# Index queries by columns for the later rows, key and head weights on their own, row squares from the input's columns

## The chip, the cores and the metric

The kernel runs on 1 core of one Trainium2 chip. The metric is the device time of one execution in microseconds (us), median of the runs. TensorE's matmuls are PE in the profile, its weight loads PEld; VectorE is DVE, ScalarE is ACT, GpSimd is POOL, SyncE is SP.

## What is computed

One decoder layer on 256 rows of width 2048, all in float32. What matters here:

```python
h = rms_norm(x, norm_gain)                 # 256 x 2048
proj = h @ w_in                            # split into qa ka va ga | qi ki wi | qb kb vb gb | ma mb
qi = apply_rope(qi.reshape(S, 16, 64)); ki = apply_rope(ki)      # index queries, one shared key
score = sum over heads of relu(qi_h . ki) * wi_h                 # 256 x 256, causal
_, sel = top_k(score, 64)                  # topk = SEQ // 4: each row attends to 64 keys of branch A
```

qi has 1024 columns of w_in, ki 64 and the head weights wi 16. A row with at most 64 keys before it (rows 0 to 63) selects all of them, whatever its scores. Branch A attends to the selected keys, branch B to all; both are gated, projected, merged and projected again.

## The kernel before

**Products.** w_in is read in units: two tiles of 128 rows of w_in (k) by up to 512 columns. Eight units (CK) make a chunk over all 2048 rows. Each operand is split into `hi`, rounded to the type in which TensorE takes a matmul of 4-byte data in one pass, and `lo`, what is left. A unit is three products (hi x hi, lo x hi, hi x lo) for 2 k tiles and 2 blocks of rows: 12 matmuls. h stands transposed (`hT_hi`, `hT_lo`) and is the stationary operand; the weights stream by as the moving one, so a chunk comes out with rows on partitions. Products for which this isn't done (the early rows' scores, the values of branch A) are plain float32.

**Order.** SP loads unit u into slot u % 4 of `raw` (a ring of four), ACT makes `hi` (`make_hi`), DVE `lo` (`make_lo`), TensorE multiplies. ACT makes unit u's `hi` only when unit u-4 is multiplied (`unit_done`), so all engines step with TensorE. The loops `for c ... for i in range(CK)` on each engine write out by hand which other work stands ahead of which unit; `make_hi_ahead(c, i)` and `make_lo_ahead(c, i)` make the unit four further on.

**The index part.** Chunks 0, 1 and 2 are 384, 384 and 336 columns wide (`IDX_W`): queries in six, and in the last four heads, the key and the head weights beside them (`KIWI` = 80 columns). Chunks 0 and 1 are interleaved at first (`FIRST_UNITS`), with the products in an order that lets them start early (`early_unit`), since x lands meanwhile. ACT takes each chunk out of PSUM to `stage`, DVE ropes it (`index_rope`), TensorE transposes it (`transpose_roped`, blocks of 128), ACT and DVE take out `qk_hi` and `qi_lo`. `index_scores` uses them much later, in chunks 12 and 14. Chunks 3 to 10 are qa, ka, qb, kb (`C_QK` = 3), each normed per head and roped (`norm_rope`) while the next is multiplied; then values, gates, merge gates, attention beside them, and the output projections.

**Row norms.** x comes transposed (`x_columns`), and is multiplied by the gain before the product; the factor 1/rms of each row (`rstd`) is applied when chunks are taken out. For it x is loaded once more by rows (`x_own`, 2 MB), and ACT squares and sums it, 2048 columns at a time.

Of the kernel before, what the change touches and what calls it, by code (L numbers as in the profile page):

```python
# [11 lines left out]
P = 128  # L31
D = 2048
# [17 lines left out]
X_OWN_AFTER = ((1, 3), (1, 5), (1, 7), (2, 1))  # L50
# [4 lines left out]
IDX_W = (384, 384, 256 + KIWI)  # L55
IDX_BLOCKS = tuple(w // P for w in IDX_W)
# [13 lines left out]
C_QK, C_V, C_G, C_M = 3, 11, 15, 19  # L70
C_O = 27
# [21 lines left out]
FIRST_UNITS = ((0, 0), (1, 0), (0, 1), (1, 1)) + tuple((c, i) for c in range(2) for i in range(2, CK))  # L93
FIRST_END = CK + 2
assert IDX_W[0] == IDX_W[1]


def chunk_end(c):
    return FIRST_END if isinstance(c, int) and c == 0 else c * CK + CK


def chunk_width(c):
    return IDX_W[c] if c < C_QK else CW

# [24 lines left out]
def chunk_bank(c):  # L129

    return 2 * ((c + 1) % 2)


def build_layer(nc, x, x_columns, positions, w_in, a_q_gain, a_k_gain, b_q_gain, b_k_gain,
# [4 lines left out]
    with ExitStack() as ctx:  # L139
# [29 lines left out]
        x_own = sb("x_own", [P, RT, D], at=qk_at + 4 * 24 * S)  # L169
# [17 lines left out]


# [6 lines left out]
        def of_four(n, part, home):  # L195
            maps = home[:, :, :].rearrange("p r (j s) -> p j r s", s=CW)
            first = {0: 0, 1: 0, 2: 4, 3: 4}[(n - C_QK) // 2] + 2 * ((n - C_QK) % 2)
            return maps[:, first:first + 2, :, part]

        def of_blocks(n, cols, home):  # L200
            at = (n - C_QK) * 4 + QA
            return home[:, at:at + 4, cols].rearrange("p (a b) s -> p a b s", b=2)
# [72 lines left out]
        tab_ci = g[:, 1, 0:128].rearrange("p (r d) -> p r d", r=RT)  # L275
        tab_si = g[:, 1, 128:256].rearrange("p (r d) -> p r d", r=RT)
# [10 lines left out]
        x_own_landed = [sem(f"x_own_landed_{r}") for r in range(RT)]  # L287
# [18 lines left out]
        index_tables_ready, tables_ready = sem("index_tables_ready"), sem("tables_ready")  # L306
        lam_sums, lam_exps = sem("lam_sums"), sem("lam_exps")
        x_squares, rstd_ready = sem("x_squares"), sem("rstd_ready")

# [22 lines left out]
        def _(sp):  # L332
# [4 lines left out]
            def load_x_own(part):  # L337
                r, at = part // 2, slice((part % 2) * (D // 2), (part % 2 + 1) * (D // 2))
                sp.dma_start(x_own[:, r, at], x_rows[:, r, at]).then_inc(x_own_landed[r], 16)

            def load_first(u, j):
                c, i = FIRST_UNITS[u]
                col = COL["qi"] + c * IDX_W[0]
                sp.dma_start(raw[:, u, j, 0:IDX_W[0]],
                             w_in[0][(2 * i + j) * P:(2 * i + j + 1) * P, col:col + IDX_W[0]]
                             ).then_inc((raw_first[u], raw_landed[u])[j], 16)

            def load(slot, u, weights, k0, col, width=CW):
# [3 lines left out]
                src = weights[0][k0 * P:(k0 + 2) * P, bass.ds(col, width)].rearrange("(k p) n -> p k n", p=P)  # L352
                sp.dma_start(raw[:, slot, :, 0:width], src).then_inc(raw_landed[slot], 16)

            def load_chunk(c, col, width=CW):
                for i in range(CK):
                    load(i % RING, c * CK + i, w_in, 2 * i, col, width)


# [3 lines left out]
            for u in range(1, EARLY):  # L363
                if u > 1:
                    load_x(u)
                load_first(u, 0)
                load_first(u, 1)
            for u in range(EARLY, 2 * CK):
# [3 lines left out]
                load(u % RING, u, w_in, 2 * i, COL["qi"] + c * IDX_W[0], IDX_W[0])  # L372
# [5 lines left out]
            rows = [(gains[:, j], row) for j, row in enumerate((a_q_gain, a_k_gain, b_q_gain, b_k_gain))]  # L378
            rows += [(lams[:, j], row) for j, row in enumerate((lambda_q1, lambda_k1, lambda_q2, lambda_k2))]
            rows += [(sub_gain[:, :], b_subln_gain)]  # L380
            for c, col in ((2, COL["qi"] + IDX_W[0] + IDX_W[1]),):
                for i in range(CK):
                    load(i % RING, c * CK + i, w_in, 2 * i, col, IDX_W[c])
                    if (c, i) in X_OWN_AFTER:
                        load_x_own(X_OWN_AFTER.index((c, i)))
                    for to, row in rows[i:i + 1] if c == 2 and i < CK - 1 else rows[i:] if c == 2 else ():
                        sp.dma_start(to, row[0].partition_broadcast(P)).then_inc(consts_landed, 16)
            with sp.Fori(0, 2) as branch:
                with sp.Fori(0, 4) as n:
                    load_chunk(C_QK + branch * 4 + n, branch * COL["qb"] + n * CW)  # L390
# [34 lines left out]
        def _(pool):  # L425
            nc.gpsimd.memset(ident[:, :], 0.0).then_inc(pool_wrote, 1)
            nc.gpsimd.memset(bias_b[:, :], 0.0).then_inc(pool_wrote, 1)
            nc.gpsimd.memset(half[:, :], -0.5).then_inc(pool_wrote, 1)
            pool.wait_ge(pool_wrote, 3)
# [57 lines left out]
            rows = [[t[:, r * 64:(r + 1) * 64] for t in (cos_t, nsin_t, sin_t)] for r in range(RT)]  # L487
            for r, (c_r, *s_r) in enumerate(rows):
                for b in range(2):
                    half_b = slice(b * 32, b * 32 + 32)  # L490
                    nc.gpsimd.tensor_copy(tab_ci[:, r, half_b], c_r[:, 0:64:2]).then_inc(index_tables_ready, 1)
                    nc.gpsimd.tensor_copy(tab_si[:, r, half_b], s_r[b][:, 0:64:2]).then_inc(index_tables_ready, 1)
# [22 lines left out]
        def _(pe):  # L515
            mm = nc.tensor.matmul

            def unit(u, slot, k0, s_hi, s_lo, bank, first, last, width=CW):

                w_hi, w_lo = (t[:, slot, :, 0:width] for t in (hi, lo))  # L520
                pe.wait_ge(lo_ready, u + 1)
                order = [(j, r) for j in range(2) for r in range(RT)]
                for j, r in order:
                    a_hi = s_hi[:, k0 + j, r * P:(r + 1) * P]
                    a_lo = s_lo[:, k0 + j, r * P:(r + 1) * P]
                    o = ps[:, bank + r, 0:width]
                    mm(o, a_hi, w_hi[:, j], start=first and j == 0, stop=False)  # L527
                    mm(o, a_hi, w_lo[:, j], start=False, stop=False)  # L528
                    ins = mm(o, a_lo, w_hi[:, j], start=False, stop=j == 1 and last)  # L529
                ins.then_inc(unit_done, 1)  # L530

            def early_unit(u):

                c, unit_k = FIRST_UNITS[u]

                def products(stationary, moving, j, first=False, last=False):
                    for r in range(RT):
                        ins = mm(ps[:, chunk_bank(c) + r, 0:IDX_W[0]], stationary[:, 2 * unit_k + j, r * P:(r + 1) * P],  # L538
                                 moving[:, u % RING, j, 0:IDX_W[0]], start=first, stop=last)
                    return ins  # L540

                for j in range(2):
                    pe.wait_ge(hi_first if j == 0 and u < EARLY else hi_ready, u + 1)
                    pe.wait_ge(x_hi_first if j == 0 and u == 0 else split_hi, unit_k + 1)
                    products(hT_hi, hi, j, first=unit_k == 0 and j == 0)
                    pe.wait_ge(x_lo_first if j == 0 and u == 0 else split_lo, unit_k + 1)
                    products(hT_lo, hi, j)
                for j in range(2):
                    pe.wait_ge(lo_first if j == 0 and u == 0 else lo_ready, u + 1)
                    ins = products(hT_hi, lo, j, last=unit_k == CK - 1 and j == 1)  # L550
                ins.then_inc(unit_done, 1)

            def w_in_unit(c, i, bank, width=CW):

                if not isinstance(c, int) or c >= 2:
                    if i == 0:
                        pe.wait_ge(chunk_out, c - 1)
# [855 lines left out]
```

## Time and profile before

| | |
|---|---|
| median of 3 runs | 798.16 us (797.63 to 798.37) |
| span of the profiled execution, first to last instruction | 796.4 us |
| PE, PEld busy | 792.7 us, 667.3 us |
| DVE, ACT, POOL busy | 481.5, 418.4, 46.8 us |
| read from HBM | 150.25 MB, 191 GB/s over the span |

The profile was taken from one execution; what lies outside its span is the difference to a run's time. A matmul's printed duration has its whole pipeline in it, so several overlap: what one costs in a stream is the distance from its start to the next one's. TensorE's granted clock is 1.00 (2.4 GHz) over the kernel.

### The profile page before, as it was taken

Reading aid. Unit: us, or ns where it says so; the run is one execution under the profiler, and the core shown is the slowest. Engines: PE = TensorE matmul, PEld = TensorE weight load, DVE = VectorE, ACT = ScalarE, POOL = GpSimd, SP = SyncE. Lnnn points to the kernel's source line nnn. Section 1 sums busy time; section 2 is a strip of 40 time slices with the busy share of each in tenths; the row PEclk is TensorE's granted clock in tenths of the full one; section 3 lists DMA queues with packets and bytes.
Section 4 is the critical chain, followed back from the end, with each engine's and each line's share of the span. In section 5 each row is a group of like instructions: output and inputs, shape, how many; then the busy total and the mean of one; then the engine's idle time right before and its main releaser. Section 6 shows DMA issues by size and latency. Waiting matters only on the chain.

```text
span 796.4 us, 10773 instructions
## 1 busy us (share of the span) xinstructions
PE 792.7 (100%) x3810; PEld 667.3 (84%) x3810; DVE 481.5 (60%) x663; ACT 418.4 (53%) x670; POOL 46.8 (6%) x70
## 2 busy tenths in 40 slices
PE   9999999999999999999999999999999999999998
PEld 9998888888888888888888888888888888888887
DVE  7677766666677554668656455555455566665453
ACT  7574556665555454556465554555575444443431
POOL 4341000000000000000000000000000000000000
PEclk9999999999999999999999999999999999999999
DMA  9986665666666565666655665655665855555563
GB/s 316 313 264 198 186 187 168 183 199 180 199 187 187 171 194 162 196 189 193 177 154 173 166 176 161 185 160 172 173 185 182 293 195 184 185 194 189 187 194 122
DMA packets 81082, 152.92 MB, mean 192 GB/s; under 512 B 5136, under 2 KB 12944, under 8 KB 80784
## 3 DMA queue, kind: packets, MB, share of 16 engines
q1 hardware_dynamic: 80752, 152.06, 62.8%
q8 instruction: 25, 0.41, 0.2%
q10 hardware_dynamic: 288, 0.30, 0.1%
q14 instruction: 17, 0.14, 0.0%
HBM read 150.25 MB, written 2.10 MB: 191 GB/s over the span
## 4 chain that ended last, share of the span: by engine, by line
PE 97%; ACT 1%; DMA 1%; SPq 0%; issue 0%; DVE 0%; ACTq 0%
PE ps L527 30%; PE ps L529 30%; PE ps L528 29%; PE ps L538 2%; PE ps L569 1%; PE ps L580 1%; DMA raw<-in_w_in 1%; PE ps L638 0%; PE ps L749 0%; PE ps L748 0%; PE ps L747 0%; PE ps L646 0%; ACT L938 0%; ACT L832 0%; ACT g L832 0%; PE ps L626 0%
## 5 line engine op out<-in xcount | busy, mean ns | idle before, releaser
L1068 DVE TENSOR_TENSOR lo<-raw,hi 128x1024 fp32r<-128x1024 f32 (+2 forms) x279 | 335.2, 1204 | 290.2 <-ACT hi L819 288.4
L819 ACT ACTIVATE hi<-raw 128x1024 fp32r<-128x1024 f32 (+2 forms) x277 | 287.1, 1040 | 337.4 <-PE ps L529 323.8
L527 PE MATMUL ps<-hi,hT_hi 128*128 128x512 f32 (+2 forms) x936 | 364.3, 389 | 0.0
L529 PE MATMUL ps<-hi,hT_lo 128*128 128x512 f32 (+2 forms) x936 | 361.1, 386 | 0.0
L528 PE MATMUL ps<-lo,hT_hi 128*128 128x512 f32 (+2 forms) x936 | 360.8, 385 | 0.0
L529 PEld LDWEIGHTS ps<-hi,hT_lo 128*128 128x128 f32 x936 | 175.7, 188 | 35.1
L528 PEld LDWEIGHTS ps<-lo,hT_hi 128*128 128x128 f32 x936 | 175.8, 188 | 32.9
L527 PEld LDWEIGHTS ps<-hi,hT_hi 128*128 128x128 f32 x936 | 175.7, 188 | 33.0
L527 PE MATMUL ps<-hi,ogT_hi 128*128 128x512 f32 x128 | 50.1, 391 | 0.0
L529 PE MATMUL ps<-hi,ogT_lo 128*128 128x512 f32 x128 | 49.8, 389 | 0.0
L528 PE MATMUL ps<-lo,ogT_hi 128*128 128x512 f32 x128 | 49.8, 389 | 0.0
L453 POOL TENSOR_SCALAR small<-small 128x8 f32<-128x8 f32 (+1 forms) x13 | 2.8, 212 | 504.2 <-ACT stage L999 318.4
L529 PEld LDWEIGHTS ps<-hi,ogT_lo 128*128 128x128 f32 x128 | 24.0, 188 | 5.0
L528 PEld LDWEIGHTS ps<-lo,ogT_hi 128*128 128x128 f32 x128 | 24.0, 188 | 4.9
L527 PEld LDWEIGHTS ps<-hi,ogT_hi 128*128 128x128 f32 x128 | 24.0, 188 | 4.9
L938 ACT ACTIVATE roped<-stage,small 128x128 f32<-128x128 f32 (+1 forms) x32 | 14.3, 446 | 13.0 <-DVE small L1206 13.0
L856 ACT ACTIVATE swapped<-stage 128x128 f32<-128x128 f32 x64 | 18.9, 297 | 0.3
L455 POOL TENSOR_TENSOR small<-small,half 128x8 f32<-128x8 f32 (+1 forms) x13 | 16.6, 1281 | 1.1
L1088 DVE TENSOR_TENSOR swapped<-stage,g 128x256 f32<-128x256 f32 (+2 forms) x44 | 16.2, 409 | 0.0
L1084 DVE TENSOR_TENSOR roped<-stage,g 128x512 f32<-128x512 f32 (+2 forms) x22 | 14.5, 660 | 0.0
L1092 DVE TENSOR_TENSOR roped<-roped,swapped 128x1024 f32<-128x1024 f32 (+2 forms) x11 | 12.3, 1121 | 0.0
L856 ACT ACTIVATION_READ_ACCUMULATOR swapped<-stage 128x1 f32 x64 | 12.0, 188 | 0.0
(167 smaller groups left out, 484.5 us busy)
## 6 DMA issues: line engine op xcount, KB each, us to landing
raw<-in_w_in SPq DMA_DIRECT2D x192, 512.0 KB, 3.8
raw<-in_w_out SPq DMA_DIRECT2D x32, 512.0 KB, 4.3
raw<-in_w_o_a SPq DMA_DIRECT2D x16, 512.0 KB, 3.7
raw<-in_w_o_b SPq DMA_DIRECT2D x16, 512.0 KB, 3.6
raw<-in_w_in SPq DMA_DIRECT2D x13, 384.0 KB, 5.3
raw<-in_w_in SPq DMA_DIRECT2D x8, 336.0 KB, 5.3
x_own<-in_x SPq DMA_DIRECT2D x4, 512.0 KB, 6.4
g<-in_x SPq DMA_DIRECT2D x1, 2048.0 KB, 10.3
```

The lines of the kernel that those rows point to most:

```text
L455: return tt(out, mean, half[:, 0:width], ALU.pow)
L527: mm(o, a_hi, w_hi[:, j], start=first and j == 0, stop=False)
L528: mm(o, a_hi, w_lo[:, j], start=False, stop=False)
L529: ins = mm(o, a_lo, w_hi[:, j], start=False, stop=j == 1 and last)
L538: ins = mm(ps[:, chunk_bank(c) + r, 0:IDX_W[0]], stationary[:, 2 * unit_k + j, r * P:(r + 1) * P], moving[:, u % RING, j, 0:IDX_W[0]], sta ...
L819: activation(hi[:, slot, :, 0:width], raw[:, slot, :, 0:width], ACT.Copy).then_inc(hi_ready, 1)
L856: ins = activation(swapped[:, r, at], stage[:, r, at], ACT.Square, accum_out=ss_h[:, j:j + 1])
L938: ins = activation(probs[buf][:, at], masked[buf][:, at], ACT.Exp, scale=SCALE, bias=neg_max[:, j:j + 1], accum_out=sum_p[:, j:j + 1])
L1068: tt(lo[:, slot, :, 0:width], raw[:, slot, :, 0:width], hi[:, slot, :, 0:width].bitcast(F32), ALU.subtract).then_inc(lo_ready, 1)
L1084: mark(tt(cos_out[:, r], src[:, r], c_tab, ALU.mult))
L1088: mark(tt(sin_out[:, r, :, half_b], src[:, r, :, other], s_tab, ALU.mult))
L1092: tt(roped[:, :, 0:cols], roped[:, :, 0:cols], swapped[:, :, 0:cols], ALU.add).then_inc(rope_done, 1)
```

## The change

- The queries are computed transposed, and for rows 64 to 255 alone (`Q_FIRST` = 64, `Q_LATE` = 192): 128 columns of w_in are the stationary operand and 192 columns of hT stream by. Two halves of 512 columns, `query_unit`, 24 matmuls a unit. ACT copies them out with halves of heads swapped (`swap_queries`), DVE ropes them in place (`query_rope`) with tables that TensorE has transposed (`transpose_tables`). No transposes of queries. Their first 64 rows are zeros, and `bias_a` is cleared for those rows ahead of the selection's use. 1/rms isn't applied to the queries, as before.
- qa's first chunk is moved to the front and interleaved with the first half of the queries; `C_QK` is now 2.
- The key and head weights (80 columns) are loaded once (`kw`), split, and multiplied in `key_products`, two k tiles ahead of each unit of chunk 3.
- The row squares come from x_columns: ACT squares eight pieces of 512, POOL adds them up (`sq`), TensorE sums over partitions (`sum_squares`). `x_own` is gone.

```diff
-IDX_W = (384, 384, 256 + KIWI)
-IDX_BLOCKS = tuple(w // P for w in IDX_W)
+Q_FIRST = TOPK
+Q_LATE = S - Q_FIRST
+QI_BLOCKS = IDX_HEADS * IDX_DIM // P // 2
...
-C_QK, C_V, C_G, C_M = 3, 11, 15, 19
-C_O = 27
+C_QK, C_V, C_G, C_M = 2, 10, 14, 18
+C_O = 26
...
-FIRST_UNITS = ((0, 0), (1, 0), (0, 1), (1, 1)) + tuple((c, i) for c in range(2) for i in range(2, CK))
-FIRST_END = CK + 2
+FIRST_UNITS = tuple((c, i) for i in range(CK) for c in range(2))
+FIRST_END = 2 * CK
+QI_BANKS = (2, 4)
...
@@ SP @@
-                if (c, i) in X_OWN_AFTER:
-                    load_x_own(X_OWN_AFTER.index((c, i)))
...
+                if i == 2:
+                    src = w_in[0][:, COL["kiwi"]:COL["kiwi"] + KIWI].rearrange("(k p) n -> p k n", p=P)
+                    sp.dma_start(kw[:, :, :], src).then_inc(kw_landed, 16)
...
@@ POOL @@
+            nc.gpsimd.memset(qkT[:, QI:QI + 2 * QI_BLOCKS, 0:Q_FIRST], 0.0).then_inc(qi_cleared, 1)
...
+            for t in range(1, CK):
+                pool.wait_ge(x_squared, t + 1)
+                mark(tt(sq[:, 0, :], sq[:, 0, :], sq[:, t, :], ALU.add))
+                settle()
+            tt(sq[:, 0, 0:S], sq[:, 0, 0:S], sq[:, 0, S:2 * S], ALU.add).then_inc(x_summed, 1)
...
@@ TensorE @@
+            def query_unit(u, i, eight):
...
+                def products(weights, moving, first=False, last=False):
+                    for j in range(2):
+                        for b in range(QI_BLOCKS):
+                            o = ps[:, QI_BANKS[eight] + b // 2, b % 2 * Q_LATE:(b % 2 + 1) * Q_LATE]
+                            ins = mm(o, weights[:, u % RING, j, b * P:(b + 1) * P], moving[:, 2 * i + j, Q_FIRST:S],
+                                     start=first and j == 0 and b % 2 == 0, stop=last and j == 1, skip_group_check=True)
+                    return ins
...
+                products(hi, hT_hi, first=i == 0)
+                products(hi, hT_lo)
+                pe.wait_ge(lo_ready, u + 1)
+                products(lo, hT_hi, last=i == CK - 1).then_inc(unit_done, 1)
+
+            def key_products(i):
+
+                if i == 0:
+                    pe.wait_ge(kw_lo_ready, 1)
+                    pe.wait_ge(tabT_ready, 1)
+                for k in (2 * i, 2 * i + 1):
+                    for r in range(RT):
+                        a_hi, a_lo = (t[:, k, r * P:(r + 1) * P] for t in (hT_hi, hT_lo))
+                        o = ps[:, S0, r * P:r * P + KIWI]
+                        mm(o, a_hi, kw_hi[:, k, :], start=k == 0 and r == 0, stop=False, skip_group_check=True)
+                        mm(o, a_hi, kw_lo[:, k, :], start=False, stop=False, skip_group_check=True)
+                        ins = mm(o, a_lo, kw_hi[:, k, :], start=False, stop=k == KT - 1, skip_group_check=True)
...
+            def transpose_tables():
...
+                pe.wait_ge(index_tables_ready, 3 * RT)
...
+            def sum_squares():
...
+                pe.wait_ge(x_summed, 1)
+                pe.wait_ge(tabT_ready, 1)
+                for r in range(RT):
+                    ins = mm(ps[:, S0 + 1, 2 * r:2 * r + 2], sq[:, 0, r * P:(r + 1) * P], ones, start=True, stop=True)
...
             for u, (c, i) in enumerate(FIRST_UNITS):
...
+                if u == 11:
+                    transpose_tables()
+                if c == 0:
+                    early_unit(u, i)
                 else:
+                    query_unit(u, i, 0)
+            for i in range(CK):
+                if i == 2:
+                    sum_squares()
+                query_unit(2 * CK + i, i, 1)
+            for c in range(C_QK + 1, C_QK + 4):
                 for i in range(CK):
+                    if i == 6:
+                        transpose_roped(c - 1 - C_QK)
+                    if c == C_QK + 1:
+                        key_products(i)
+                    if (c, i) == (C_QK + 3, 2):
+                        transpose_index_key()
+                    w_in_unit(c, i, chunk_bank(c))
...
@@ ScalarE @@
+                if c == 1:
+                    square_x(i)
+                if u == 11:
                     act.wait_ge(reduced, 1)
                     activation(sin_t, ang, ACT.Sin).then_inc(sin_ready, 1)
...
+                    if c in (C_QK, C_QK + 1) and i < 4:
+                        swap_queries(c - C_QK, i)
+                    if c in (C_QK, C_QK + 1) and i == 6:
+                        queries_hi(c - C_QK)
+                    if (c, i) == (C_QK, 6):
+                        act.wait_ge(kw_landed, 16)
+                        activation(kw_hi[:, :, :], kw[:, :, :], ACT.Copy).then_inc(kw_hi_ready, 1)
...
@@ VectorE @@
+                    if c in (C_QK, C_QK + 1) and 4 <= i <= 5:
+                        for step in ((0, 1), (2,))[i - 4]:
+                            query_rope(c - C_QK, step)
+                    if c in (C_QK, C_QK + 1) and i == 7:
+                        query_rope(c - C_QK, 3)
+                    if (c, i) == (C_QK, 7):
+                        dve.wait_ge(kw_hi_ready, 1)
+                        tt(kw_lo[:, :, :], kw[:, :, :], kw_hi[:, :, :].bitcast(F32), ALU.subtract).then_inc(kw_lo_ready, 1)
...
+                        mark(nc.vector.memset(bias_a[0:Q_FIRST, 0:P], 0.0))
```

`query_rope` has four steps: two products from PSUM with the cosines and one of `qi_swap` with the sines (the third signals `qi_read`), the sum (256 elements into `qkT`, 512 in `qi_rope`), and later the low part (512). `swap_queries` copies one quarter of the partitions, 768 elements.

## Rows read from the trace of the kernel before

**Rows 1.** Page of the profile, busy time and the chain that ended last.

```profile
PE 792.7 (100%) x3810; PEld 667.3 (84%) x3810; DVE 481.5 (60%) x663; ACT 418.4 (53%) x670; POOL 46.8 (6%) x70
...
PE 97%; ACT 1%; DMA 1%; SPq 0%; issue 0%; DVE 0%; ACTq 0%
```

**Rows 2.** Index part: PE, PEld, DVE, ACT, POOL busy, granted clock, DMA share, GB/s.

```profile
4.68:54.53 49.85, 49.77 (x302) 49.29 (x301) 38.34 (x59) 36.78 (x59) 18.48 (x29) 1.00 0.96 310
```

**Rows 3.** Groups by shape, TensorE, 4.6 to 54.6 us: the index products.

```profile
L538 PE MATMUL ps<-hi,hT_hi 128*128 128x384 f32 x40 | 10.6, 345 | 0.1
L527 PE MATMUL ps<-hi,hT_hi 128*128 128x336 f32 x32 | 10.2, 320 | 0.0
...
L527 PE MATMUL ps<-hi,hT_hi 128*128 128x384 f32 x24 | 8.0, 334 | 0.0
```

**Rows 4.** Timeline of TensorE: start us, us, line, shape; five stretches.

```profile
33.01 0.33 PE L527 MATMUL ps<-hi,hT_hi 128*128 128x384 f32 x1
...
38.55 0.34 PE L529 MATMUL ps<-hi,hT_lo 128*128 128x384 f32 x1
...
52.69 0.32 PE L527 MATMUL ps<-hi,hT_hi 128*128 128x336 f32 x1
...
54.38 0.32 PE L529 MATMUL ps<-hi,hT_lo 128*128 128x336 f32 x1
...
72.12 0.39 PE L527 MATMUL ps<-hi,hT_hi 128*128 128x512 f32 x1
...
83.92 0.39 PE L528 MATMUL ps<-lo,hT_hi 128*128 128x512 f32 x1
...
487.37 0.28 PE L665 MATMUL ps<-qk_hi,swapped_r 128*128 128x256 f32 x1
...
488.32 0.28 PE L667 MATMUL ps<-qk_hi,pT_lo 128*128 128x256 f32 x1
...
405.75 0.38 PE L653 MATMUL ps<-v,swapped 128*128 128x128 f32 x2
405.97 0.39 PE L654 MATMUL ps<-v,swapped 128*128 128x128 f32 x2
```

**Rows 5.** Timeline of TensorE's weight loads after short work, two places.

```profile
93.82 0.19 PEld L527 LDWEIGHTS ps<-hi,hT_hi 128*128 128x128 f32 x1
93.92 0.19 PEld L528 LDWEIGHTS ps<-lo,hT_hi 128*128 128x128 f32 x1
...
262.33 0.19 PEld L527 LDWEIGHTS ps<-hi,hT_hi 128*128 128x128 f32 x1
262.44 0.19 PEld L528 LDWEIGHTS ps<-lo,hT_hi 128*128 128x128 f32 x1
```

**Rows 6.** Timeline of TensorE: six index transposes and the matmul behind them.

```profile
38.73 0.63 PE L569 MATMUL ps<-ident_r,roped_r 128*128 128x128 f32 x6
39.20 0.39 PE L527 MATMUL ps<-hi,hT_hi 128*128 128x336 f32 x1
```

**Rows 7.** Groups by shape, ACT and DVE, 4.6 to 60 us.

```profile
L819 ACT ACTIVATE hi<-raw 128x1024 fp32r<-128x1024 f32 x5 | 5.3, 1058 | 1.8 <-PE ps L529 1.3 <-DMA raw<-in_w_in 0.5
...
L1068 DVE TENSOR_TENSOR lo<-raw,hi 128x1024 fp32r<-128x1024 f32 x5 | 6.7, 1340 | 3.6 <-ACT hi L819 3.6
...
L1092 DVE TENSOR_TENSOR roped<-roped,swapped 128x768 f32<-128x768 f32 x2 | 1.9, 948 | 0.0
L1137 DVE TENSOR_TENSOR g_r<-ps,qk_hi 128x384 fp32r<-128x384 f32 x2 | 1.1, 549 | 0.0
```

**Rows 8.** Timeline of ACT in the chunk from 77 us: a split that waits.

```profile
85.31 1.06 ACT L819 ACTIVATE hi<-raw 128x1024 fp32r<-128x1024 f32 x1 [1.56 <-PE ps L529]
```

**Rows 9.** Timeline of POOL: two table products of one size.

```profile
50.91 1.74 POOL L500 TENSOR_TENSOR g<-v 128x256 f32<-128x256 f32 x1
...
57.67 0.74 POOL L500 TENSOR_TENSOR g<-v 128x256 f32<-128x256 f32 x1
```

**Rows 10.** Timeline of TensorE: its first product of weights.

```profile
4.68 0.80 PE L538 MATMUL ps<-hi,hT_hi 128*128 128x384 f32 x2
```

More of the change, by code:

```diff
@@ L371, in _ @@
                     load_x(i + 1)
[L372 removed]
+                load(u % RING, u, w_in, 2 * i, COL[("qa", "qi")[c]])
                 if u == EARLY + 1:
                     sp.dma_start(pos_i[:, :], positions).then_inc(phases_landed, 16)
[L375 to L390 removed]
+                if u >= 2 * CK - 4:
+                    load_row(u - (2 * CK - 4))
+            for i in range(CK):
+                load(i % RING, 2 * CK + i, w_in, 2 * i, COL["qi"] + CW)
+                if i < 5:
+                    load_row(4 + i)
+                if i == 2:
+                    src = w_in[0][:, COL["kiwi"]:COL["kiwi"] + KIWI].rearrange("(k p) n -> p k n", p=P)
+                    sp.dma_start(kw[:, :, :], src).then_inc(kw_landed, 16)
+            with sp.Fori(1, 4) as n:
+                load_chunk(C_QK + n, n * CW)
+            with sp.Fori(0, 4) as n:
+                load_chunk(C_QK + 4 + n, n * CW + COL["qb"])
             for c, name in ((C_V, "va"), (C_V + 2, "vb"), (C_G, "ga"), (C_G + 2, "gb")):
@@ L516, in _, with unit @@
             mm = nc.tensor.matmul
-            def unit(u, slot, k0, s_hi, s_lo, bank, first, last, width=CW):
-                w_hi, w_lo = (t[:, slot, :, 0:width] for t in (hi, lo))
+            def unit(u, slot, k0, s_hi, s_lo, bank, first, last):
                 pe.wait_ge(lo_ready, u + 1)
@@ L549, in early_unit @@
                     pe.wait_ge(lo_first if j == 0 and u == 0 else lo_ready, u + 1)
-                    ins = products(hT_hi, lo, j, last=unit_k == CK - 1 and j == 1)
+                    ins = products(hT_hi, lo, j, last=i == CK - 1 and j == 1)
                 ins.then_inc(unit_done, 1)
[L553 to L557, printed above, removed]
-                    unit(c * CK + i, i % RING, 2 * i, hT_hi, hT_lo, bank, i == 0, i == CK - 1, width)
@@ L562, in transpose_roped, with w_in_unit @@
+            def w_in_unit(c, i, bank):
+                if i == 0:
+                    if isinstance(c, int) and c == C_QK + 1:
+                        pe.wait_ge(qi_read, 1)
+                    else:
+                        pe.wait_ge(chunk_out, taken_out(c - 2))
+                unit(c * CK + i, i % RING, 2 * i, hT_hi, hT_lo, bank, i == 0, i == CK - 1)
+            def transpose_roped(n):
                 pe.wait_ge(rope_done, n + 1)
-                if not isinstance(n, int) or n > 0:
+                if isinstance(n, int) and n == 0:
+                    pe.wait_ge(qi_read, 2)
+                else:
@@ new lines, in queries_hi, with key_out @@
+            def queries_hi(eight):
+                act.wait_ge(qi_roped, eight + 1)
+                first = QI + eight * QI_BLOCKS
+                activation(qk_hi[:, first:first + QI_BLOCKS, P:S], qi_rope[:, :, P - Q_FIRST:Q_LATE],
+                           ACT.Copy).then_inc(qi_hi_ready, 1)
+            def key_out():
+                act.wait_ge(kw_done, 1)
+                act.wait_ge(rstd_ready, 1)
+                for r in range(RT):
+                    ins = activation(kst[:, r, :], ps[:, S0, r * P:r * P + KIWI], ACT.Copy, scale=rstd[:, r:r + 1])
+                ins.then_inc(kst_out, 1)
```

446 lines of the change are left out of this document (238 added, 208 removed).

## The prediction

> **What bounds the kernel now.** I read the page first. TensorE is busy 100% of the span and 97% of the chain that ended last is its matmuls [rows 1]; VectorE at 60% and ScalarE at 53% are covers. So whatever adds or takes TensorE time moves the end one for one, and every other engine counts only if it makes TensorE wait. Then I asked for the stretch of the index projection, from the first product of weights to the first 512-wide chunk: 49.85 us, no idle TensorE to speak of, granted clock 1.00, DMA at 96% of its engines but still ahead [rows 2]. The reader is to see that the stretch is a plain sum of matmuls: three products of 40 + 24 matmuls of 384 columns, three of 32 of 336 columns [rows 3], so 192 and 96.
>
> The duration printed for a matmul (0.33 to 0.39) contains its pipeline; what counts is the distance from start to start. 32 distances at 384 columns take 5.54 us, 0.173 each; 11 at 336 take 1.69, 0.154; 52 at 512 take 11.80, 0.227; 8 at 256 take 0.95, 0.119 [rows 4]. That is 0.42 ns a column and 12 ns for each matmul (0.227 - 0.173 over 128 columns, and the rest). 192 x 0.173 + 96 x 0.154 = 33.2 + 14.8 = 48.0 us. That is what is replaced.
>
> The price of a narrow matmul is not in that line, for each one also loads its own 128x128 weights, and at 256 columns and more this is hidden. Where a load finds the spare place free, two follow one another by 0.10 and by 0.11 us [rows 5] (93.82 to 93.92, behind short transposes; 262.33 to 262.44, behind the index scores). And the plain f32 products of 128 columns, which show two records and two loads each, take 0.22 us a pair, again 0.11 a load [rows 4]. So below some 230 columns I expect the load to set the pace.
>
> **The change, part by part.**
>
> *Query products.* 2 halves x 8 units x 24 = 384 matmuls of 192 columns. By columns each would be 12 + 192 x 0.42 = 0.093 us; by the load 0.11. The load is the longer, so 384 x 0.11 = 42.2 us.
>
> *Key and head weights on their own.* 16 row tiles x 2 x 3 = 96 matmuls of 80 columns, which until now rode along in the 336-wide ones for 80 x 0.42 = 34 ns each, 3.2 us in all. Alone, each costs a load: 96 x 0.11 = 10.6 us. Together 52.8 against 48.0: **+4.8 us**. This is the heart of it: a quarter of the columns goes (106,000 to 81,400), but the number of matmuls goes from 288 to 480. Bounds of the price: 0.105 from the shorter distance between loads, 0.12 if the 12 ns of every matmul come on top of the load (which is the 256-wide row): 480 x 0.105 = 50.4 (+2.4), 480 x 0.12 = 57.6 (+9.6). I take 0.11, since the plain f32 pairs show it in a stream.
>
> The two distances of rows 5 agree with the Trainium skill, "TensorE: Matmul & The Clock Gate", section "LDWEIGHTS (loading the stationary operand)", which gives columns over 1.2 GHz, 107 ns for 128; by it 480 x 0.107 = 51.4 us would be the two parts, +3.4.
>
> *Transposes.* Six take 0.47 us until the next matmul starts (38.73 to 39.20) [rows 6], 0.078 each. 18 (16 of queries, 2 of keys) become 6 (4 of tables, 2 of keys): **-0.9**.
>
> *Row squares.* Two plain f32 products of 2 columns, four loads: **+0.4**. The two ScalarE squares of 2048 columns and x_own's 2 MB go, eight squares of 512 come. DMA and ScalarE there don't bound [rows 1, 2]: nothing. Its cover gone would show as ScalarE splitting late; rings of four units (10 us) stand between.
>
> *qa's first chunk* only moves to the front; its 96 matmuls stay 512 wide: nothing. At the start the first transfers are a third larger (512 for 384 columns) and TensorE begins at 4.68 us when they are there [rows 10]: I estimate **+0.3**, 0 to 1.
>
> *A new wait.* key_products(0) stands in TensorE's order at the head of chunk 3 and waits for kw_lo. Who makes that? Unit n's split on ScalarE (1.06 us for 1024 elements [rows 7]) starts only when unit n-4 is done; the ones of today wait for just that, 1.56 us [rows 8]. In chunk 2, with U24 the end of its last unit: kw_hi (1280 elements, by the 1.06 of 1024 some 1.3 us) stands ahead of the split at i=6, which can start at U23 at the earliest and ends at U23 + 1.1, or 1.4 with queries_hi and kw_hi ahead of it (they start after the split of i=5, U22 + 1.1). VectorE then does that unit's lo (1.2 us by 0.95 for 768, 1.34 beside a busy POOL), the queries' low part (0.7 by 0.55 for 384) and kw_lo (1.4) [rows 7]: U23 + 4.7. A query unit lasts 24 x 0.11 = 2.6 us, so kw_lo is ready at U24 + 2.0, and TensorE stands from U24 on. **+2.0**, from 0 (if VectorE runs ahead) to 3.5. Behind that wait in TensorE's queue is the whole of chunk 3; no one else is hurt, since hi and lo of its units are made meanwhile.
>
> *Other waits.* The first rope of queries has to have read banks 2 and 3 before chunk 3: five units of slack. Transposing qa waits for the second half's rope, but chunk 3 lasts 8 x 1.3 us longer by its key products, more than VectorE's added 2.1 us there (two of 0.55 from PSUM, one of 0.95) [rows 7]. On POOL seven sums of 512 elements precede sum_squares in unit 18, near 53 us. A 256-element product takes 0.74 or 1.74 us, the long ones beside a busy VectorE [rows 9]; so 1.3 to 3 us each. They follow the tables, which follow the sines that ScalarE does after the split of unit 11, so once unit 7 has ended (5 + 4 x (2.7 + 2.6) = 26 us): I estimate 33 us. They end between 43 and 55, and unit 18 starts at 5 + 8 x 5.3 + 2 x 2.6 = 53: mostly in time, and up to 2 us late, for which I leave room in the high bound. The memset of qkT (512 elements) lies in POOL's long wait for positions; the two small VectorE operations by the selection lie ahead of the scores they serve: nothing.
>
> Sum: 4.8 - 0.9 + 0.4 + 0.3 + 2.0 = **+6.6 us**. The profiled execution's span is 796.4, the runs' median 798.16, 1.8 of it outside the span; the forecast is 803.0 for the span, 804.8 for the median. Its own range: +1.9 (price 0.105, no stall, no late start) to +13.6 (0.12, waits of 3.5 in all, start 1): 800 to 812.
>
> **Rivals.**
>
> *Columns decide (ends faster).* If the weight load overlaps wholly with the matmuls before it, several ahead, the pace is 0.093 us at 192 and 0.046 at 80: 35.7 + 4.4 = 40.1 us, -7.9; with the other terms -6.1 us, 792; without the stall 790. It decides once the 480 matmuls cost under 0.096 us on average, where the sum is zero. For it: nothing ever paces TensorE at 256 columns but the columns [rows 4]. Against it: rows 5, where the next load starts only 0.10 to 0.11 after the last although its matmul had begun. By the Trainium skill, "TensorE: Matmul & The Clock Gate", section "Back-to-back issue gap", the distance is N/2.4 + 2.5 ns, 82.5 for 192 and 36 for 80; 31.7 + 3.4 us would be the two parts, and the kernel about 11 us faster. The same section allows more for pairs of load and matmul, and rows 4 already show 119 where it has 109 for 256.
>
> *Narrow rounded products run as plain f32 does.* The narrowest product on split operands in the trace has 256 columns. Plain f32 takes 0.22 for 128 columns [rows 4], four times a column's price. If 192-wide ones fell to that: 384 x 0.33 + 96 x 0.22 = 148 us, +100, 898 us, and no stall for kw. For it only that the trace shows no narrow one; against it that transposes of such operands at 128 columns take 0.078 [rows 6].
>
> *Nothing much.* Price near 0.10 and no stall cancel with the transposes: within 1.6 us of 798.
>
> **Chances.** The load decides 0.72; columns decide 0.12; as plain f32 0.10; cancels 0.06. Under 0.2% (1.6 us) no measurement of this kernel tells from no change. Faster 0.13, same 0.05, slower 0.82. The range takes in the likeliest case and the fast one, 791 to 812, and leaves out the 898.
>
> **What the changed profile would show.** Distance of 0.11 between 192-wide and between 80-wide matmuls alike, with PEld without gaps (right), or 0.093 and 0.046 (columns), or two records each (plain f32). One TensorE gap of some 2 us before the first 80-wide matmul, released by VectorE's kw_lo. sum_squares without a wait for POOL. From chunk 4 on the same distances as now. A different price of a load in a stream, or a drop of the granted clock from 1.00 beside the narrow products, would make the sum wrong.

## The result, and the profile after

The changed kernel takes 811.12 us (median of 4, 810.49 to 811.70), the kernel before 797.97 us in the runs beside it (797.63 to 798.37). The ratio is 1.0166, 95% interval 1.0152 to 1.0180: 13.2 us slower. The forecast was 804.8, slower with 0.82, range 791 to 812. Sign and mechanism came as forecast; the loss is twice the +6.6 us of the sum, at the upper end of the likeliest case's own range (800 to 812). The profiled execution's span is 808.6 us, 12.2 more than before's 796.4; the steps below are counted against that.

The page of the kernel after (busy time, granted clock in 40 slices, chain that ended last by engine), to be held against [rows 1]:

```profile
span 808.6 us, 11086 instructions
PE 801.3 (99%) x3994; PEld 675.1 (83%) x3994; DVE 485.3 (60%) x645; ACT 421.2 (52%) x667; POOL 65.0 (8%) x77
PEclk9998999999999999999999999999999999999999
PE 96%; ACT 2%; DVE 1%; issue 0%; ACTq 0%
```

Two things are new. TensorE's share of the chain is one per cent lower, ScalarE's and VectorE's together two per cent higher: somewhere TensorE waited. And the fourth slice of the granted clock (61 to 81 us) is below full. The waits of the first 110 us name one place (engine and line, what it waited for: us in total, times, longest):

```profile
PE ps L596 <- DVE kw_lo L1305: 3.6, 1, 3.6
```

Two stretches of the kernel after (columns as in [rows 2]):

```profile
4.68:71.50 66.82, 66.82 (x490) 62.20 (x488) 50.20 (x49) 45.30 (x64) 43.49 (x41) 1.00 0.85 268
75.16:81.67 6.51, 6.51 (x22) 5.70 (x23) 1.08 (x1) 2.22 (x16) 1.87 (x2) 0.51 0.48 148
```

Up to 71.5 us, with qa's chunk and all queries in it, TensorE stands nowhere and the granted clock is 1.00. Behind the wait it is 0.51, which is the lower level, 1.2 GHz; from the next slices of the page on it is full again. TensorE's timeline shows the start, the narrow products, the row squares, the wait and what follows it (start us, us, line, shape, and in brackets the idle time before and its releaser):

```profile
4.89 1.22 PE L553 MATMUL ps<-hi,hT_hi 128*128 128x512 f32 x2
...
13.89 1.03 PE L576 MATMUL ps<-hT_hi,hi 128*128 128x192 f32 x8
...
54.88 0.53 PE L617 MATMUL ps<-const-float32-1.0,sq 128*128 128x2 f32 x4
55.27 0.90 PE L576 MATMUL ps<-hT_hi,hi 128*128 128x192 f32 x6
...
60.69 1.05 PE L576 MATMUL ps<-hT_hi,hi 128*128 128x192 f32 x8
61.58 1.05 PE L576 MATMUL ps<-hT_lo,hi 128*128 128x192 f32 x8
...
70.51 1.05 PE L576 MATMUL ps<-hT_hi,lo 128*128 128x192 f32 x8
75.16 0.44 PE L596 MATMUL ps<-kw_hi,hT_hi 128*128 128x80 f32 x1 [3.59 <-DVE kw_lo L1305]
...
77.74 0.77 PE L542 MATMUL ps<-hi,hT_hi 128*128 128x512 f32 x1
...
81.67 0.40 PE L542 MATMUL ps<-hi,hT_hi 128*128 128x512 f32 x1
...
82.61 0.29 PE L596 MATMUL ps<-kw_hi,hT_hi 128*128 128x80 f32 x1
82.72 0.28 PE L597 MATMUL ps<-kw_lo,hT_hi 128*128 128x80 f32 x1
...
83.61 0.47 PE L542 MATMUL ps<-hi,hT_hi 128*128 128x512 f32 x1
83.93 0.39 PE L543 MATMUL ps<-lo,hT_hi 128*128 128x512 f32 x1
```

and, from the kernel before, the first product behind its fourth group of 12:

```profile
13.77 0.51 PE L538 MATMUL ps<-hi,hT_hi 128*128 128x384 f32 x2
```

Read by distances, start to start, as the prediction did:

- Eight query products of 192 columns take 0.89 us (60.69 to 61.58), 0.111 each. 384 of them are 42.7 us. The narrow key products lie 0.11 apart too (82.61 to 82.72), although they have 80 columns. A group of 12 takes 1.25 us (82.36 to 83.61), since the first follows a 512-wide product whose long stay hides part of its load; the 96 are 10.1. The first 512-wide product behind each group then takes 0.32 (83.61 to 83.93) and not 0.23: 0.7 for the eight. Together 53.5 where 48.0 stood: +5.5.
- The row squares take 0.39 us (54.88 to 55.27), with no wait: +0.4. Twelve transposes fewer: -0.9.
- The start: the first product at 4.89, not 4.68 [rows 10]. Up to 13.89, 24 products of 512 columns and 24 of 192 take 9.0 us where their steady distances make 8.13, 0.87 too much. Before, the first 48 products of 384 columns took 9.09 (4.68 to 13.77) where 48 x 0.173 is 8.3, 0.77 too much. Together 0.2 + 0.87 - 0.77 = +0.3.
- The wait: eight products from 70.51 end their turn at 71.4, and the next starts at 75.16. +3.75.
- The granted clock after the wait: 12 key products take 2.58 us (75.16 to 77.74), 0.213 apart instead of 0.112, +1.2. Nine 512-wide ones take 3.93 (77.74 to 81.67) instead of 9 x 0.227 and the 0.09 of the first, 2.13, +1.8. Together +3.0.

5.5 + 0.4 - 0.9 + 0.3 + 3.75 + 3.0 = 12.05 of the 12.2 us. Who was late for the wait is seen on the other engines. VectorE of the kernel after, then ScalarE, then POOL:

```profile
63.18 1.02 DVE L1218 TENSOR_TENSOR qi_rope<-ps,idx_tabT 128x384 f32<-128x384 f32 x2
...
65.29 1.75 DVE L1175 TENSOR_TENSOR lo<-raw,hi 128x1024 fp32r<-128x1024 f32 x1
66.97 0.95 DVE L1228 TENSOR_TENSOR qkT<-qi_rope,qi_swap 128x256 f32<-128x256 f32 x1
67.85 1.22 DVE L1229 TENSOR_TENSOR qi_rope<-qi_rope,qi_swap 128x512 f32<-128x512 f32 x1
...
71.87 1.22 DVE L1175 TENSOR_TENSOR lo<-raw,hi 128x1024 fp32r<-128x1024 f32 x1 [1.12 <-ACT hi L917]
...
73.62 1.48 DVE L1305 TENSOR_TENSOR kw_lo<-kw,kw_hi 128x1280 fp32r<-128x1280 f32 x1
```

```profile
69.10 0.64 ACT L948 ACTIVATE qk_hi<-qi_rope 128x512 fp32r<-128x512 f32 x1 [1.74 <-DVE qi_rope L1229]
69.64 1.26 ACT L1027 ACTIVATE kw_hi<-kw 128x1280 fp32r<-128x1280 f32 x1
```

```profile
35.43 13.07 POOL L506 TENSOR_TENSOR sq<-sq 128x512 f32<-128x512 f32 x7
48.59 1.60 POOL L508 TENSOR_TENSOR sq<-sq 128x256 f32<-128x256 f32 x1
...
61.42 0.73 POOL L516 TENSOR_TENSOR g<-v 128x256 f32<-128x256 f32 x1
```

kw_lo is the last of VectorE's list, as forecast. But ScalarE's `queries_hi` stood 1.74 us for its input `qi_rope`, and `kw_hi` and the split behind it, from 70.80 on, moved with it. `qi_rope` was late because VectorE's operations from 65.29 on ran while POOL made the head's tables (61.42 to 72.2): the low part took 1.75 us instead of the 1.22 it takes at 71.87, the sum of 256 elements 0.95 (the same line took 0.42 for the second half, with POOL idle), the one of 512 took 1.22 (0.69). Each of the three is 0.53 longer, 1.6 us in all. With the one at 64.23, which took 1.14 instead of the 0.96 of its twin at 98.16, that is 1.8 us, all of ScalarE's wait of 1.74.

### The profile page after: what moved, and what is told of

The parts are those of the page before. It is cut to its first block, busy times and chain, and to the rows that moved or that the text cites. A ratio compares the mean times of both kernels' runs of the same rounds, so it can differ in the third digit from the quotient of the medians.

```text
span 808.6 us, 11086 instructions
## 1 busy us (share of the span) xinstructions
PE 801.3 (99%) x3994; PEld 675.1 (83%) x3994; DVE 485.3 (60%) x645; ACT 421.2 (52%) x667; POOL 65.0 (8%) x77
## 4 chain that ended last, share of the span: by engine, by line
PE 96%; ACT 2%; DVE 1%; issue 0%; ACTq 0%
PE ps L542 27%; PE ps L544 27%; PE ps L543 27%; PE ps L576 4%; PE ps L553 3%; PE ps L643 1%; PE ps L660 1%; PE ps L666 1%; ACT hi L917 1%; PE ps L597 0%; PE ps L598 0%; PE ps L596 0%; PE ps L733 0%; PE ps L843 0%; PE ps L842 0%
## 5 line engine op out<-in xcount | busy, mean ns | idle before, releaser
L1175 DVE TENSOR_TENSOR lo<-raw,hi 128x1024 fp32r<-128x1024 f32 x271 | 336.5, 1245 | 295.9 <-ACT hi L917 294.3
L917 ACT ACTIVATE hi<-raw 128x1024 fp32r<-128x1024 f32 x269 | 283.5, 1058 | 345.4 <-PE ps L544 326.4
L542 PE MATMUL ps<-hi,hT_hi 128*128 128x512 f32 x848 | 334.8, 395 | 0.0
L544 PE MATMUL ps<-hi,hT_lo 128*128 128x512 f32 x848 | 331.1, 390 | 0.0
L543 PE MATMUL ps<-lo,hT_hi 128*128 128x512 f32 x848 | 331.1, 390 | 0.0
L544 PEld LDWEIGHTS ps<-hi,hT_lo 128*128 128x128 f32 x848 | 159.6, 188 | 34.1
L576 PE MATMUL ps<-hT_hi,lo 128*128 128x192 f32 x128 | 16.9, 274 | 0.0
L576 PE MATMUL ps<-hT_lo,hi 128*128 128x192 f32 x128 | 16.9, 274 | 0.0
L576 PE MATMUL ps<-hT_hi,hi 128*128 128x192 f32 x128 | 16.8, 274 | 0.0
L576 PEld LDWEIGHTS ps<-hT_hi,hi 128*128 128x128 f32 x128 | 16.1, 191 | 0.5
```

The source lines that it names most:

```text
L542: mm(o, a_hi, hi[:, slot, j, :], start=first and j == 0, stop=False)
L543: mm(o, a_hi, lo[:, slot, j, :], start=False, stop=False)
L544: ins = mm(o, a_lo, hi[:, slot, j, :], start=False, stop=j == 1 and last)
L576: ins = mm(o, weights[:, u % RING, j, b * P:(b + 1) * P], moving[:, 2 * i + j, Q_FIRST:S], start=first and j == 0 and b % 2 == 0, stop=las ...
L917: activation(hi[:, slot, :, :], raw[:, slot, :, :], ACT.Copy).then_inc(hi_ready, 1)
L1175: tt(lo[:, slot, :, :], raw[:, slot, :, :], hi[:, slot, :, :].bitcast(F32), ALU.subtract).then_inc(lo_ready, 1)
```

## The experiments

**Undo the lateness of kw alone.** ScalarE's split moves four units ahead, and VectorE's with it:

```diff
@@ ScalarE @@
-                    if (c, i) == (C_QK, 6):
+                    if (c, i) == (C_QK, 2):
                         act.wait_ge(kw_landed, 16)
@@ VectorE @@
-                    if (c, i) == (C_QK, 7):
+                    if (c, i) == (C_QK, 3):
                         dve.wait_ge(kw_hi_ready, 1)
```

> The split of the key and head weights is made four and five units earlier (their transfer had landed near 48 us). Theory: the wait of 3.6 us goes, and with it the half clock that followed it (about 3.0 us), so 6.6 us less than the changed kernel, near 804.5, ratio to the kernel before 1.008. Rival 1: the half clock comes from the narrow products and not from the wait: it stays, 3.6 us less, 807.5. Rival 2: another late step of VectorE takes the wait's place: less than 3 us gained, with a TensorE gap of over 1 us elsewhere.

Measured: 803.56 us (803.45 to 803.97), ratio to before 1.0068 (1.0051 to 1.0085), 7.6 us under the kernel after; span 802.0. TensorE's timeline at the same place:

```profile
70.50 1.05 PE L576 MATMUL ps<-hT_hi,lo 128*128 128x192 f32 x8
71.40 0.22 PE L596 MATMUL ps<-kw_hi,hT_hi 128*128 128x80 f32 x1
71.45 0.28 PE L597 MATMUL ps<-kw_lo,hT_hi 128*128 128x80 f32 x1
```

The first key product starts at 71.40 instead of 75.16, the next ones follow 0.11 apart at full clock, and no wait of TensorE is left. The spans differ by 6.6, the two terms above make 6.75. (The medians differ by 7.6, because the changed kernel's profiled execution was its shortest run.) So one late input of 1280 elements cost more than half of the whole loss. What is left, +5.6 of span, is the products, the start, the squares and the transposes: 5.5 + 0.3 + 0.4 - 0.9 = 5.3.

**Idle time, or narrow products, as the cause of the lower clock.** The wait stays, and TensorE multiplies zeros into an unused part of a bank meanwhile:

```diff
                 if i == 0:
+                    for _ in range(16):
+                        mm(ps[:, S0 + 1, P:2 * P], zeros, zeros, start=True, stop=True)
                     pe.wait_ge(kw_lo_ready, 1)
```

> The wait stays, but 16 products of zeros (3.5 us) stand in it. Theory: the idle time is what lowered the clock, so it stays at 1.00 after it: 3.0 us less than the changed kernel, near 808. Rival: the narrow products lower it, so nothing changes (811).

Measured: 807.57 us (807.50 to 807.81), ratio 1.0119 (1.0102 to 1.0136); span 805.6. Its timeline, and below it the stretch around it:

```profile
71.15 3.76 PE L591 MATMUL ps<-const-float32-0.0 128*128 128x128 f32 x32
74.90 0.30 PE L598 MATMUL ps<-kw_hi,hT_hi 128*128 128x80 f32 x1
75.03 0.28 PE L599 MATMUL ps<-kw_lo,hT_hi 128*128 128x80 f32 x1
```

```profile
71.00:90.00 19.00, 19.00 (x126) 17.09 (x126) 11.87 (x15) 11.64 (x27) 2.79 (x4) 1.00 0.48 140
```

The same narrow products stand here, no earlier than VectorE allows, but the clock stays at 1.00, and the span is 3.0 under that of the kernel after. The first 12 key products and nine 512-wide ones behind them take 3.51 us instead of 6.51. So it was the idle TensorE and not the narrowness of what follows that brought the lower level, and its price is 3.0 us, beside the wait's own 3.6 (805.6 against 802.0 for the first experiment).

**Load or columns as the pace.** Two widths beside the kernel's 192. In one, all but the first query product of each block have 128 columns; in the other all have 256:

```diff
@@ 128 columns @@
+                            width = Q_LATE if first else P
+                            o = ps[:, QI_BANKS[eight] + b // 2, (b % 2 + 1) * Q_LATE - width:(b % 2 + 1) * Q_LATE]
+                            ins = mm(o, weights[:, u % RING, j, b * P:(b + 1) * P], moving[:, 2 * i + j, S - width:S],
@@ 256 columns @@
+                            o = ps[:, QI_BANKS[eight] + b // 2, b % 2 * S:(b % 2 + 1) * S]
+                            ins = mm(o, weights[:, u % RING, j, b * P:(b + 1) * P], moving[:, 2 * i + j, 0:S],
```

> The query products take 128 columns in place of 192 (all but the first product of each block; the queries of 64 rows are left incomplete). Theory, the weight load sets the pace: distances stay at 0.111 us, total within 0.5 us of the changed kernel. Rival, columns set it: 368 x 64 x 0.42 ns = 9.9 us less.

> The query products take all 256 columns (what is read of them afterwards is at the wrong places). Theory, the load sets the pace up to some 230 columns: distance 0.119, 384 x 0.008 = 3.1 us more than the changed kernel, 814.2. Rival, columns: 384 x 64 x 0.42 ns = 10.3 us more, 821.

Measured: 810.37 us (810.20 to 811.46) for 128 columns, 813.10 (812.45 to 813.62) for 256; ratios 1.0157 (1.0140 to 1.0174) and 1.0190 (1.0173 to 1.0207). TensorE's timeline of the one with 128, then of the one with 256:

```profile
60.81 1.06 PE L577 MATMUL ps<-hT_hi,hi 128*128 128x128 f32 x8
61.70 1.06 PE L577 MATMUL ps<-hT_lo,hi 128*128 128x128 f32 x8
```

```profile
60.69 1.12 PE L576 MATMUL ps<-hT_lo,hi 128*128 128x256 f32 x8
61.65 1.12 PE L576 MATMUL ps<-hT_hi,lo 128*128 128x256 f32 x8
```

Eight products of 128 columns take 0.89 us, as those of 192 do; eight of 256 take 0.96. A third fewer columns bring 0.75 us between medians whose runs overlap (0.1 between the spans), where the rival had 9.9. A third more cost 2.0, where the columns alone would make 10.3. The 2.0 are less than the 3.1 expected: the wait for kw_lo was 0.3 shorter there (3.29 us), the start and the stretch at the lower clock 0.4 shorter each. The load of 128 weight columns is the pace; the rival "columns decide" is out at every width of this change. The figure by the Trainium skill, "TensorE: Matmul & The Clock Gate", section "LDWEIGHTS (loading the stationary operand)", that the prediction cites is 0.107 us a load; in this stream it is 0.111.

**Key and head weights stationary.** With kw early as in the first experiment, the 80 columns of kw are loaded and the 256 rows of the input stream past them. 48 products take the place of 96; the result is transposed back in two steps:

```diff
-                    for r in range(RT):
-                        a_hi, a_lo = (t[:, k, r * P:(r + 1) * P] for t in (hT_hi, hT_lo))
-                        o = ps[:, S0, r * P:r * P + KIWI]
-                        mm(o, a_hi, kw_hi[:, k, :], start=k == 0 and r == 0, stop=False, skip_group_check=True)
...
+                    o = ps[0:KIWI, S0, 0:S]
+                    mm(o, kw_hi[:, k, :], hT_hi[:, k, :], start=k == 0, stop=False)
+                    mm(o, kw_lo[:, k, :], hT_hi[:, k, :], start=False, stop=False)
+                    ins = mm(o, kw_hi[:, k, :], hT_lo[:, k, :], start=False, stop=k == KT - 1)
...
+            def transpose_keys():
+
+                pe.wait_ge(kT_ready, 1)
```

> On top of the earlier split of the key and head weights (803.6): these 80 columns become the stationary operand and 256 columns of h stream by, 48 products in place of 96, two more transposes bring the result back to rows. Theory (the number of products times the longer of load and columns): 48 x 0.119 = 5.7 in place of the 10.1 us that the 96 took, plus 0.2, so 4.3 us less, 799.3. Rival: the narrow products cost little because each unit's first one hides behind a wide matmul, and the gain stays under 2 us.

Measured: 798.58 us (11 runs, 798.35 to 798.87), before 797.92 (21 runs), ratio 1.0007 (0.9998 to 1.0016); span 796.9. Its timeline:

```profile
71.32 0.28 PE L597 MATMUL ps<-hT_hi,kw_hi 128*80 128x256 f32 x1
71.44 0.28 PE L598 MATMUL ps<-hT_hi,kw_lo 128*80 128x256 f32 x1
...
72.03 0.40 PE L545 MATMUL ps<-hi,hT_hi 128*128 128x512 f32 x1
72.26 0.40 PE L546 MATMUL ps<-lo,hT_hi 128*128 128x512 f32 x1
```

0.119 apart, the 48 take 5.65 us in all instead of 10.1, and the 512-wide product behind each group is back at 0.23, another 0.7. Less some 0.2 for the two new transposes that is 5.0 of the 5.1 by which the span falls against the first experiment. Half as many products with three times the columns each is faster: the price is per product, not per column.

**Fewer and wider query products.** On top of that, for two of each unit's four blocks, hi x hT_hi and hi x hT_lo are one product of 384 columns, over a tile that holds both parts of the input. The second result has its own columns of PSUM and is added by VectorE after a ScalarE copy. The row squares move one unit ahead, into a bank that is still free:

```diff
+            def pairs(first):
+                    for j in range(2):
+                        for b in range(2):
+                            o = ps[:, QI_BANKS[eight] + b, 0:2 * Q_LATE].rearrange("p (n s) -> p n s", n=2)
+                            mm(o, hi[:, u % RING, j, b * P:(b + 1) * P], hT_both[:, :, 2 * i + j, Q_FIRST:S],
...
+                activation(qi_rope[:, 0:2, :], ps[:, bank:bank + 2, Q_LATE:2 * Q_LATE], ACT.Copy).then_inc(qi_copied, 1)
...
+                    two = ps[:, bank:bank + 2, 0:Q_LATE]
+                    tt(qi_rope[:, 0:2, :], two, qi_rope[:, 0:2, :], ALU.add).then_inc(qi_summed, 1)
```

> On top of the keys stationary: for two of the four blocks of each query unit the high weights are loaded once for both high and low columns of h (one product of 384 columns in place of two of 192), in PSUM columns of their own; ScalarE copies the second part out and VectorE adds it. Theory: 64 products become 64 fewer loads, each pair 0.173 in place of 0.222: 3.1 us less, 796.1, faster than the kernel before by 0.25%. Rival: the longer chain on ScalarE and VectorE makes TensorE wait at the head of a chunk, and the gain is gone (799 or more).

Measured: 797.60 us (11 runs, 797.11 to 798.25), ratio 0.9997 (0.9988 to 1.0006); span 795.4. Its timeline shows what the pairs gave and what the longer way of the queries took:

```profile
29.39 0.87 PE L586 MATMUL ps<-hT_both,hi 128*128 128x384 f32 x4
30.09 1.03 PE L592 MATMUL ps<-hT_both,hi 128*128 128x192 f32 x8
...
90.52 0.85 PE L669 MATMUL ps<-ident_r,roped_r 128*128 128x128 f32 x8 [1.08 <-DVE qi_swap L1270]
```

This lies between the theory's 796.1 and the rival's 799. The 64 pairs take 11.7 us and the other 256 products 28.2, 39.9 instead of 42.7. The span falls by 1.5 only: TensorE stands 1.08 us before qa's transposes, for VectorE. After this idle time the 256-wide products are 0.12 apart at once (91.36, 91.47, 91.59 in the same timeline) and the granted clock stays at its upper level.

**Give that wait more cover.** qa's transposes go one unit later:

```diff
-                    if i == 6:
+                    if i == (7 if c == C_QK + 1 else 6):
                         transpose_roped(c - 1 - C_QK)
```

> The kernel with pairs (797.6), qa's transposes one unit later in TensorE's order. Theory: their wait of 1.2 us for the second half's rope goes, 796.4, 0.2% under the kernel before. Rival: what waits for the transposes (ScalarE's copies, then the next chunk's) is late in its turn and the time stays 797.6.

Measured: 795.85 us (10 runs, 795.33 to 796.39), before 797.68 beside it (20 runs), ratio 0.9976 (0.9967 to 0.9985); span 794.0. The wait is gone and this version beats both kernels, the one before by 1.8 us:

```profile
92.66 0.81 PE L669 MATMUL ps<-ident_r,roped_r 128*128 128x128 f32 x8
93.30 0.31 PE L614 MATMUL ps<-hT_both,kw_hi 128*80 128x256 f32 x1
```

39.9 + 5.65 = 45.5 us of products stand where 48.0 stood, -2.5; with -0.9, +0.4, and +0.2 for the two transposes of the keys, -2.8. The span is 2.4 shorter than before's; the start is not in this sum.

**The row squares by themselves.** The kernel before, with only this part of the change: ScalarE squares the columns in chunk 1, POOL adds, TensorE sums across partitions; x_own isn't loaded:

```diff
@@ POOL @@
+            for t in range(1, CK):
+                pool.wait_ge(x_squared, t + 1)
+                mark(tt(sq[:, 0, :], sq[:, 0, :], sq[:, t, :], ALU.add))
+                settle()
+            tt(sq[:, 0, 0:S], sq[:, 0, 0:S], sq[:, 0, S:2 * S], ALU.add).then_inc(x_summed, 1)
@@ TensorE @@
+                    if (c, i) == (2, 3):
+                        pe.wait_ge(x_summed, 1)
+                        for r in range(RT):
+                            ins = mm(ps[:, S0 + 1, 2 * r:2 * r + 2], sq[:, 0, r * P:(r + 1) * P], ones, start=True, stop=True)
@@ ScalarE @@
+                    if c == 1:
+                        tiles = xt[:, X_FRONT + 2 * i * S:X_FRONT + (2 * i + 2) * S]
+                        activation(sq[:, i, :], tiles, ACT.Square).then_inc(x_squared, 1)
```

> The kernel before with one part of the change alone: row squares from the input's columns, eight squares of 512 on ScalarE, the sums on POOL, two narrow products on TensorE; x isn't loaded by rows. Theory: 0.4 us more (the two products), 798.5, within the noise. Rival 1: POOL's sums come late, TensorE waits, 1 to 3 us more. Rival 2: 2 MB less in the stretch where DMA is at 96% takes waits off: up to 0.8 us less.

Measured: 803.97 us (5 runs, 803.83 to 804.14), ratio 1.0075 (1.0062 to 1.0089), 6 us slower where +0.4 was expected; span 802.4. VectorE's timeline of this kernel, then POOL's and TensorE's:

```profile
33.36 1.65 DVE L1086 TENSOR_TENSOR roped<-stage,g 128x384 f32<-128x384 f32 x1
34.92 2.83 DVE L1090 TENSOR_TENSOR swapped<-stage,g 128x192 f32<-128x192 f32 x2
```

```profile
29.36 11.09 POOL L487 TENSOR_TENSOR sq<-sq 128x512 f32<-128x512 f32 x7
```

```profile
43.24 0.97 PE L566 MATMUL ps<-ident_r,roped_r 128*128 128x128 f32 x6 [4.37 <-DVE roped L1094]
```

The expectation fell. TensorE waits 4.37 us before six transposes, for VectorE's ropes, which ran beside POOL's seven sums; behind it the next products are again slow (0.28 apart at 336 columns instead of the 0.154 of [rows 4], at a granted clock of 0.50 for 3.0 us). The wait, 1.3 us at the lower clock and the 0.4 of the squares make up the 6.0 of span. The expectation's rival of a late sum fell too: the sums were done at 41.2 us and needed at 50.7. The theory formed on this: two tensor operations, one of POOL and one of VectorE, slow each other down. The rival: the sums have nothing to do with it, and ScalarE's eight squares or the moved loads make the ropes late.

**The same without the seven sums.** The wait for the squares stays, and POOL makes only the last addition, so that the norms come from two of the 16 tiles:

```diff
-            for t in range(1, CK):
-                pool.wait_ge(x_squared, t + 1)
-                mark(tt(sq[:, 0, :], sq[:, 0, :], sq[:, t, :], ALU.add))
-                settle()
+            pool.wait_ge(x_squared, CK)
```

> The kernel before with the row squares from the input's columns, as in the last run, but the seven POOL sums of 512 elements left out (the row norms are then those of two tiles only). Theory: VectorE's ropes took up to three times as long beside them (1.65 for 0.55 us at 384 columns), so without them TensorE's gap of 4.7 us and the half clock behind it go: 5.5 us less, 798.4. Rival: the eight ScalarE squares ahead of the splits are what is late: the gap stays, 804.

Measured: 798.29 us (10 runs, 797.86 to 798.73), before 797.68 (20 runs), ratio 1.0008 (0.9999 to 1.0017); span 796.2. VectorE's timeline of this kernel at the ropes:

```profile
32.50 0.55 DVE L1083 TENSOR_TENSOR roped<-stage,g 128x384 f32<-128x384 f32 x1
32.97 0.62 DVE L1087 TENSOR_TENSOR swapped<-stage,g 128x192 f32<-128x192 f32 x2
```

With the squares, the loads and the transposes all in place, 0.55 instead of 1.65 and 0.62 instead of 2.83: the sums were the cause, and the other parts cost 0.6 us (1.4 at the end of the interval). The Trainium skill, "GPSIMD Engine Reference", section "Specifications", says that the SBUF interfaces are shared with VectorE, with contention for its instructions with two SBUF inputs; the trace agrees, since all of these read two SBUF tiles, while the two products that read PSUM at 63.18 us of the kernel after, beside a busy POOL, took 1.02, no more than at 97.11 us with POOL idle.

## Why the prediction was right, and where its size was off

- *Products, +4.8:* right in the price, 0.111 at 192 columns and 0.11 at 80; the term measured +5.5. The 0.7 on top is the 512-wide product behind each group of key products, which the prediction did not price. The widths of 128 and 256 show the load as the cause.
- *Transposes, -0.9, and row squares, +0.4:* right by their own instructions in this kernel.
- *POOL's sums in time:* right in time, 50.2 us for a need at 54.9, but the prediction asked only whether the sums would be late. It never asked whom they slow down. In the changed kernel their cover was luck: from 35.4 to 50.2 VectorE had only low parts (of the units and of the input) to make, with a ring of four units between it and TensorE, while in the kernel before the ropes stood there and the same sums cost 6 us.
- *Start, +0.3:* +0.3 by the distances. 0.2 of it is the later first product. That the longer first distances nearly cancel between the two kernels (0.87 and 0.77) was not foreseen, and no experiment takes them apart.
- *A new wait, +2.0 (0 to 3.5):* the step that was mis-sized. Place, cause and releaser were as forecast, but it measured 3.75. The working took VectorE's durations with one exception from places where POOL was idle, and let `queries_hi` start when ScalarE was free. In the trace it started when `qi_rope` was ready, 1.7 us later, after 1.6 us of stretched VectorE work beside POOL's table products. That POOL stretches such work is shown by the last two experiments at another place; that it made up the whole excess here was read from durations only. The same step held that nobody else is hurt behind the wait; TensorE's clock was.
- *Granted clock:* named as a danger beside the narrow products and not priced. It came, but from the wait, not from the products. +3.0 in the trace, 3.0 by the experiment that fills the wait. So of the 5.6 us by which the span's loss passed the sum (12.2 against 6.6), 3.0 are this term, 1.75 the wait and 0.7 the products.
- *The range, 800 to 812 for the likeliest case:* that 811.1 lies inside is in part luck. The high bound had +9.6 for the products, which needed 5.5, and 3.5 for the wait, which took 3.75. The room kept for a dearer product was filled by the lower clock, for which no bound had anything.
- *Rivals:* "columns decide" and "as plain f32" both fell by the 0.111. (The first without its stall is 790 by its own sum; the stated range begins at 791.) "Nothing much" fell for this kernel, but was within reach: kw early and its weights stationary bring the time back to 0.07% above before.

## What to carry to other kernels

At 192 columns and fewer, count weight loads and not columns: 480 narrow products cost more than the 288 wide ones, though they have a quarter fewer columns, 368 cost less, and the narrow operand was cheaper on the stationary side. A new input for a saturated TensorE should be ready well ahead of its use (four units earlier was enough here), since the wait of 3.6 us was paid twice, the second time as 3.0 us at the lower clock. And before a tensor operation is given to an idle POOL, look at what VectorE does in that stretch, not only at when POOL is done.

## What the runs showed of the hardware

- The weight load follows the granted clock. 80-wide products with 128-column loads lie 0.111 apart at the upper level and 0.213 at the lower; the loads themselves are printed with 0.19 and 0.33 us. The Trainium skill, "TensorE: Matmul & The Clock Gate", section "LDWEIGHTS (loading the stationary operand)", gives the columns over 1.2 GHz, 107 ns for 128, and names no clock level; the trace is near it at the upper level and at twice that at the lower.
- 3.6 us of idle TensorE after 67 us of full load were followed by about 6.5 us at 0.51 of the clock. In the run with 128 columns, after the same wait, it was 5.3 us at 0.50, and after the 4.4 us of the kernel with only the row squares 3.0 us at 0.50. 1.1 us of idle time in the kernel with pairs brought none. Products of zeros in the idle time kept it up.
- What a VectorE operation with two SBUF inputs loses beside a busy POOL was a fixed time for each operation, and not a share of its length. Beside POOL's products of 256 elements (65.3 to 69.1 us of the kernel after), operations of 256, 512 and 1024 elements were each 0.53 us longer: 0.42 to 0.95, 0.69 to 1.22, 1.22 to 1.75. Beside POOL's additions of 512 elements (the kernel before with the row squares), those of 192 and 384 were each 1.1 us longer, 0.31 to 1.4 and 0.55 to 1.65, and in the kernel after those of 1024 up to 1.05 longer. So short operations lose most in proportion. Why the amount is what it is, these runs don't show.
- POOL's additions of 512 elements took 13.07 / 7 = 1.87 us each beside VectorE's low parts, and 11.09 / 7 = 1.58 beside its ropes.
